# The first four expert gathers, moved from between the query product's slabs to behind its last one

## The reference

```python
def block(hb):                                   # 128 tokens, twice
    q = (hb @ w_query).reshape(PEER_BLOCK, PEER_HEADS, 2, D_KEY // 2)
    s = jnp.einsum('thpc,hpnc->thpn', q, sub_keys).astype(jnp.float32)
    top_s, top_i = lax.top_k(s, PEER_TOPK)
    ...
    best_s, best_j = lax.top_k(cand_s, PEER_TOPK)
    idx = jnp.take_along_axis(cand_i, best_j, axis=-1)
    g = jax.nn.softmax(best_s, axis=-1)
    u_sel = jnp.take(u, idx, axis=0)
    a = jax.nn.gelu(jnp.einsum('thkd,td->thk', u_sel, hb), approximate=False)
    v_sel = jnp.take(v, idx, axis=0)
    return jnp.einsum('thk,thkd->td', (g * a).astype(hb.dtype), v_sel)
```

## Time and profile before

| | |
|---|---|
| time, median of 3 runs (lowest to highest) | 3610.52 us (3609.63 to 3612.21) |
| the profiled execution: its time, its span from first to last instruction | 3617.24 us, 3615.4 us |
| PE busy | 2585.3 us (72%) |
| POOL busy | 2572.5 us (71%) |
| DVE busy | 1597.9 us (44%) |
| ACT busy | 1140.0 us (32%) |
| mean granted TensorE clock | 0.851 of full speed |
| gathers (queue q0): bytes, share of 16 DMA engines over the span | 536.97 MB, 35.3% |

### The profile page before, as it was taken

One profiled execution on the slowest core, in us unless ns is written; L12 is line 12 of the kernel. 1 busy time (PEld: TensorE's weight loads), 2 busy tenths in 40 slices (PEclk: granted clock), 3 DMA queues, 4 the chain that ended last, 5 costly groups with the idle time before them and its releaser, 6 DMA issues.

```text
span 3615.4 us, 42712 instructions
## 1 busy us (share of the span) xinstructions
PE 2585.3 (72%) x15849; PEld 2022.3 (56%) x15849; DVE 1597.9 (44%) x2168; ACT 1140.0 (32%) x2129; POOL 2572.5 (71%) x1835
## 2 busy tenths in 40 slices
PE   7996696988999999979998888802720670273067
PEld 5875485778988998869995567801310220131022
DVE  4002457123210121020004422697879779787954
ACT  5442422454444444444445754400000000000000
POOL 7887604857989998978884037888588568757852
PEclk9997797999999999989999579956975895696589
DMA  5665300435655665546563024599999999999998
GB/s 178 181 200 150 111 4 2 147 116 153 185 174 189 181 185 175 185 127 178 172 176 99 1 95 150 190 426 427 427 428 427 427 427 427 428 427 427 427 427 348
DMA packets 239890, 867.96 MB, mean 240 GB/s; under 512 B 18594, under 2 KB 20772, under 8 KB 173028
## 3 DMA queue, kind: packets, MB, share of 16 engines
q0 software_dynamic: 73776, 536.97, 35.3%
q1 hardware_dynamic: 163414, 316.11, 28.7%
q10 hardware_dynamic: 2540, 12.75, 1.2%
HBM read 860.24 MB, written 2.10 MB: 239 GB/s over the span
## 4 chain that ended last, share of the span: by engine, by line
PE 49%; POOL 23%; DMA 10%; DVE 8%; issue 6%; ACT 3%; DVEq 0%; POOLq 0%; SPq 0%; ACTq 0%
PE acc L1636 21%; PE acc L1631 19%; DMA zone<-in_peer_v,zone 10%; POOL zone L675 9%; POOL lasting L675 9%; POOL w_lo L559 5%; PE acc L1727 2%; PE acc L2085 2%; PE acc L1904 1%; DVE x_lo L1150 1%; DVE lasting L1573 1%; PE acc L1891 1%; DVE zone L1294 1%; PE acc L1984 0%; DVE zone L1425 0%
## 5 line engine op out<-in xcount | busy, mean ns | idle before, releaser
L559 POOL TENSOR_TENSOR w_lo<-lasting,w_hi 128x512 fp32r<-128x512 f32 (+1 forms) x1184 | 1574.9, 1346 | 473.3 <-ACT w_hi L721 439.4
L721 ACT ACTIVATE w_hi<-lasting 128x512 fp32r<-128x512 f32 (+1 forms) x1184 | 744.0, 633 | 955.8 <-PE acc L1631 501.5
L2085 PE MATMUL acc<-zone,lasting 128*128 128x512 f32 x512 | 258.2, 663 | 701.9 <-ACT lasting L1112 639.9
L2085 PEld LDWEIGHTS acc<-zone,lasting 128*128 128x128 f32 x512 | 106.0, 213 | 853.5 <-ACT lasting L1112 500.5
L1636 PE MATMUL acc<-x_hi,w_hi 128*128 128x256 f32 (+1 forms) x2112 | 344.7, 285 | 20.8 <-DVE x_lo L1150 14.5
L1636 PE MATMUL acc<-x_lo,w_hi 128*128 128x256 f32 (+1 forms) x2112 | 341.1, 284 | 0.0
L1636 PE MATMUL acc<-x_hi,w_lo 128*128 128x256 f32 (+1 forms) x2112 | 340.7, 284 | 0.0
L675 POOL DMA_INDIRECT zone<-in_peer_v,zone x128 | 190.3, 1486 | 176.0 <-DVE lasting L1573 77.0
L1543 DVE CUSTOM_DVE_ANT_0 zone<-lasting,zone 128x2048 f32<-128x2048 f32 x128 | 293.4, 2292 | 31.4 <-DMA lasting<-in_peer_u,zone 22.3
L1636 PEld LDWEIGHTS acc<-x_hi,w_hi 128*128 128x128 f32 x2112 | 292.2, 191 | 23.2 <-DVE x_lo L1150 11.2
L1543 DVE CUSTOM_DVE_ANT_0 zone<-zone 128x2048 f32<-128x2048 f32 x128 | 293.4, 2292 | 21.6 <-DMA zone<-in_peer_u,zone 13.7
(11 more groups left out here) (372 smaller groups left out, 3712.4 us busy)
## 6 DMA issues: line engine op xcount, KB each, us to landing
lasting<-in_w_in SPq DMA_DIRECT2D x200, 512.0 KB, 3.6
lasting<-in_w_up SPq DMA_DIRECT2D x128, 512.0 KB, 3.7
lasting<-in_w_down SPq DMA_DIRECT2D x128, 512.0 KB, 4.0
lasting<-in_w_mix_out SPq DMA_DIRECT2D x32, 512.0 KB, 3.7
lasting<-in_w_out SPq DMA_DIRECT2D x32, 512.0 KB, 3.8
lasting<-in_peer_w_query SPq DMA_DIRECT2D x32, 512.0 KB, 3.9
lasting<-in_w_kv_cross SPq DMA_DIRECT2D x16, 512.0 KB, 3.9
lasting<-in_w_q_cross SPq DMA_DIRECT2D x8, 512.0 KB, 3.3
```

The lines of the kernel that those rows point to most:

```text
L559: pool.tensor_tensor(w_lo[:, k, 0:width], ring[:, slot, s % SLOT_SLABS, 0:width], w_hi[:, k, 0:width].bitcast(FP32), ALU.subtract).then_in ...
L721: act.activation(w_hi[:, s % PARTS, 0:width], ring[:, slot, s % SLOT_SLABS, 0:width], ACT.Copy).then_inc(hi_ready, 1)
L2085: last = pe.matmul(bank(4 * t + c), diag[:, n // 2, k], rows_buf[2 * n + k][:, c * CHUNK:(c + 1) * CHUNK], start=hx % 2 == 0 and i == 0 an ...
```

## The change

The four early gathers are no longer issued between slabs. `rests` loses its parameter, the loop no longer leaves out pairs 0 and 1, and so POOL issues all sixteen gathers of the first round behind the wait for the product's last slab. No instruction is added or removed otherwise; the gathers, their order among themselves, their buffers and their waits for experts and for used buffers are the same.

```diff
-            def rests(*names, after={}):
+            def rests(*names):
...
                                 pool.tensor_tensor(w_lo[:, k, 0:width], ring[:, slot, s % SLOT_SLABS, 0:width],
                                                    w_hi[:, k, 0:width].bitcast(FP32), ALU.subtract).then_inc(lo_ready, 1)
-                                if (c, s) in after:
-                                    after[c, s]()
                     loop(pool, g.bodies, body)
...
-            early = [(n, k) for n in range(2) for k in range(2)]
-            rests("query", after={(3, 7 + 2 * e): lambda n=n, k=k: gather(0, 0, n, k) for e, (n, k) in enumerate(early)})
+            rests("query")
             chunk_done(pool, G["query"], 3)
             for phase in range(len(EXPERT_PHASES)):
                 for i in range(ROUNDS):
                     for n in range(PAIRS_OF_ROWS):
-                        if phase == 0 and i == 0 and n < 2:
-                            continue
                         if phase == 0 and i == 0 and n == 6:
                             pool.wait_ge(s_sp, 4)
                         for k in range(2):
```

## The result

| | before | change |
|---|---|---|
| median (lowest to highest) | 3610.93 us (3608.99 to 3617.36, 9 runs) | 3620.36 us (3613.81 to 3623.34, 9 runs) |
| ratio to before, 95% interval | | 1.0022 (1.0011 to 1.0032) |
| the profiled execution: time, span | 3617.24, 3615.4 us | 3620.18, 3618.4 us |
| mean granted TensorE clock | 0.851 | 0.850 |

The change is slower by about 8 us, with an interval from 4 to 12 us. Forecast was 3612.8 us, within 3609.2 to 3617.6 us. The two profiled executions stand only 3.0 us apart.

The account below looks back on a forecast made before the run. The prediction took PE and POOL to pace the products and saturated DMA transfers the expert phase; +9.82 - 6.21 - 1.37 = +2.2 us on the 3610.52 us median gave 3612.8 us, range 3609.2 to 3617.6 us.

Parts of the forecast that it names:

- Term 1: Expert phase: the four moved gathers' transfers lose their cover and join the saturated DMA queue, +9.8 us.
- Term 2: Query product's last chunk: without gathers between POOL's subtractions the product ends earlier, -6.2 us (bounds 4.1 to 8.6 us).
- the chunk before, which has no gathers in it: Query product: its last eight slabs took 13.31 us against 19.52 us in the last chunk, difference 6.21 us.
- Term 3: Just behind the product: the first gather issues faster, with no DVE dot product running, -1.4 us (bounds 0 and 1.37 us).
- My outer bound of +5.7 us: Whole change: the upper bound of the summed effect, 9.82 - 4.1 - 0 us.
- The rival "slower": End of query product: the product doesn't end earlier, so +8.5 us, 3619.0 us; chance 5%.

## Why the prediction was wrong

The measured 3620.36 us is 7.6 us above the forecast. Two inputs failed. The base was low: 3.8 us, if the median of the 35 later runs is the kernel's. And terms 2 and 3 were sized from one profile of before: by the four profiles their sum with term 1 is +2.4 us or +5.3 us, where I had +2.2 us. That leaves 0.6 to 3.6 us of the 7.6 us unexplained.

**What bounds the kernel: right.** In all fourteen profiles the expert phase is saturated (from 2400 to 3590 us a share of 1.01 and 425 to 427 GB/s), and from the seam on only the start of the transfers and the bytes left count. The kernel with the gathers behind the last subtraction shows the one-for-one relation.

**Term 1, +9.8 us for four uncovered transfers: right.** The cleanest pair is the change against the dots held until the third pair, since in both the first eight gathers behind the product take 1.04 us or less. The ends lie 1317.25 - 1308.40 = 8.85 us apart. The change's product ends 1.2 us earlier, so that the four transfers cost 10.0 us. The forecast had 9.82 us.

**Term 2, -6.2 us for the earlier end of the product: right for one of two levels.** Against the slower level it is 6.2 us. Against the faster one it is 42.09 - 37.73 = 4.4 us. This is the step that failed: "the chunk before, which has no gathers in it" was a sound yardstick for the change, and the change hit it; but the chunk with gathers was read from a single execution and taken for the kernel. I also laid most of the hold on the gathers' issue. The runs with the dots kept away show that without them the four issues delay the product by 38.95 - 37.73 = 1.2 us. The other 3 to 5 us come from DVE's dot products, which hold up the fourth gather and the last two subtractions.

**Term 3, -1.4 us for the quicker first gather: right for the same level only.** In the faster level the fifth gather already takes 0.95 us, so there is nothing to win there, and the term is its own lower bound, 0. Counted from the product's end to the end of all, the slower level takes 1.5 us more than the kernel with the dots held longer (1270.93 against 1269.46 us); the faster level takes 0.1 us less in one profile and 0.8 us more in the other.

With each level's own values the sum is +9.82 - 6.24 - 1.37 = +2.2 us against the slower level (measured 1317.25 - 1314.90 = 2.35 us) and +9.82 - 4.4 - 0 = +5.4 us against the faster (measured 4.7 and 5.9 us, 5.34 us on average). The working was sound and its inputs were one draw of two. That the first sum met the profile so closely is luck in part: the profile of before happened to show the slower level. My outer bound of +5.7 us held that average, but as an unlikely end rather than as what two of four profiles show.

**The base, 3610.52 us: too low.** The median of three runs was taken for the kernel's, with their own 2.6 us as the spread. Over 35 runs before has a median of 3614.36 us and a spread of 13 us. The change's median was nearly the same both times (3620.36 and 3619.43 us); it is before's that moved. So of the 9.4 us between the first medians, 2.4 to 5.3 us are the change's seam. The intervals of both ratios (4 to 12 us, 1.4 to 8 us) overlap the seam's cost. That the rest is chance in the base is argued from this and not shown by a run, and it would be an unlikely chance: before's nine runs at the first measurement had a median of 3610.93 us, and of random draws of nine from the 85 later executions of the same kernel some 2 in 100 have one as low. What makes the stages ahead of the query product differ by up to 7 us between executions (the start of chunk 1's key scores) is still open; it shows in kernels with and without the change. Nor does the order of two starts explain all of before's spread: in the four later series its executions have a standard deviation of 3.7 to 5.4 us. That of the four kernels with the gathers moved or the dots held longer is 1.5 to 2.1 us, that of the change 3.3 and 2.2 us; but the kernel with the dots held to the product's end, whose seam is steady, has 3.5 us.

**The rival "slower".** Its time, 3619.0 us, was closest to the measurement, by luck, and its mechanism is refuted: the product did end earlier, in both profiles of the change, with no wait of PE for POOL among its last eight slabs.

**A reason that was wrong without harm.** I wrote that from the ninth gather on POOL was held back by the queue, from gathers of 2.15 and 2.19 us. It is DVE: with the dots held to the product's end the second gather behind it already takes 2.10 us, and with the dots held longer eight in a row take 0.94 us. POOL isn't outrunning the DMA by a factor of two once dot products run; a gather every 2.4 us is just about the DMA's pace. In the profile of the change the first long issue (2.44 us at 2345.86 us) stands right behind the first dot product (2345.19 us).

**The rule on the shared port.** In the prediction I weighed the Trainium skill, "SBUF — State Buffer", section "Who interferes with whom". Its inference is that a two-input DVE instruction doesn't hold descriptor generation. Taken for a gather's whole issue, as I took it, that disagrees with the measurement: 0.95 us against 3.05 us for a gather that starts 0.01 us ahead or 0.06 us behind a dot product. It doesn't refute the inference itself, because a gather also reads its 128 indices from SBUF, and the same section has a GpSimd instruction that reads SBUF held by such a DVE instruction. The profiles show that what is held lies at the gather's start: behind its first hundredths of a microsecond the gather at 2326.87 us in the faster profile of before ran beside a dot product throughout and took 0.95 us. Whether that is the reading of the indices, no run here shows.

The section also says, of VectorE's two-port modes, that whoever issues first gets the shared pair for the whole instruction and the other blocks. For dot products and subtractions the traces agree, in both directions: the dot products took 3.15 us in place of 2.29 us, the pair of subtractions 5.93 us in place of 2.53 us. For a gather they don't: it holds up no dot product that starts behind it (2.31 us). And DVE's comparison in the last block of this document started 0.48 us ahead of the first of four subtractions, yet ended 0.56 us behind the last.

## What to carry to other kernels

When an edit changes what runs beside what on two engines that hold each other up, read the seam from several profiles of the kernel before, from a fixed event just ahead of it: one profile shows one order of two starts that lie hundredths of a microsecond apart. An early issue is worth what it covers minus what it holds up, and if another engine's work answers to that early issue at once, that work belongs in the sum: here keeping the consumer back by some 15 us won 4 us (interval 0.4 to 6.5 us), and moving the issue alone 2 to 3 us, not clear of the noise. Take the base and its spread from as many runs as there are before trusting a margin of 0.2%.

## What the hardware showed that I had not expected

- A gather's issue on GpSimd takes 0.94 us alone and about 2.1 us when DVE runs dot products of 128x2048 back to back, up to 3.05 us when it starts just behind one. Between 2300 and 2540 us of the fourteen profiles 888 gathers start 0.06 us or more into a dot product, and every one ends 0.80 to 0.84 us behind that dot product's end. In the expert phase this makes POOL's issue (2.1 us and 0.30 us of gap) nearly as slow as the transfer (2.454 us).
- DVE is held up too, by POOL's subtractions. In the kernel with the gathers where POOL has slack, DVE's comparisons of 128x512 elements, 0.69 us at their shortest in the profile of before, took 6.03 and 6.19 us beside POOL's subtractions, the first of them until all four of a series were done:

```profile
2319.94 6.03 DVE L1529 TENSOR_TENSOR zone<-zone 128x512 f32<-128x512 f32 x1
2326.01 0.69 DVE L1530 TENSOR_TENSOR zone<-zone 128x512 f32<-128x512 f32 x1
...
2327.46 6.19 DVE L1529 TENSOR_TENSOR zone<-zone 128x512 f32<-128x512 f32 x1
...
2320.42 4.99 POOL L559 TENSOR_TENSOR w_lo<-lasting,w_hi 128x512 fp32r<-128x512 f32 x4
```

- One kernel, unaltered, gave executions from 3605.68 to 3621.51 us in twelve runs, 0.44%, of which the order of two starts in its seam explains 3.6 us by the four profiles.
